# Two-layer hybrid transformer step with PEER experts: one lookup per pick for both expert tables, and gelu, gates and diagonal sums on TensorE in groups of four

## What is computed

```python
def one_chunk(xc):                       # 128 tokens, 1024 wide
    q = (xc @ wq).reshape(P_CHUNK, P_HEADS, 2, P_HALF)
    sc = jnp.einsum('thcd,hcnd->thcn', q, sub_keys)
    s1, i1 = lax.top_k(sc[:, :, 0], P_TOPK)
    s2, i2 = lax.top_k(sc[:, :, 1], P_TOPK)
    ...
    top_s, pos = lax.top_k(cand, P_TOPK)         # 8 heads x 16 picks of 16384 experts
    eidx = jnp.take_along_axis(cand_idx, pos, axis=-1)
    gate = jax.nn.softmax(top_s, axis=-1).astype(xc.dtype)
    u = jnp.take(u_tab, eidx, axis=0)
    act = jax.nn.gelu(jnp.einsum('thkd,td->thk', u, xc))
    vv = jnp.take(v_tab, eidx, axis=0)
    return jnp.einsum('thk,thkd->td', gate * act, vv)
```

## Time and profile before

| | |
|---|---|
| median of 3 runs | 2635.54 us |
| the profiled execution's own span | 2775.9 us |
| PE busy | 1502.5 us (54%) |
| DVE busy | 1580.1 us (57%) |
| ACT busy | 284.8 us (10%) |
| POOL busy | 1580.2 us (57%) |
| DMA moved | 963.23 MB, mean 347 GB/s |
| mean granted TensorE clock | 0.719 of full |

### The profile page before, as it was taken

The page is one execution under the profiler, slowest core; times in us unless marked ns, Lnnn a source line. Parts: engine busy times, 40 slices in busy tenths (PEclk is TensorE's granted clock), DMA queues, the critical chain, the costliest instruction groups (busy, mean ns, idle before and its releaser), DMA issues.

```text
span 2775.9 us, 21719 instructions
## 1 busy us (share of the span) xinstructions
PE 1502.5 (54%) x6476; PEld 657.2 (24%) x6476; DVE 1580.1 (57%) x3734; ACT 284.8 (10%) x736; POOL 1580.2 (57%) x1601
## 2 busy tenths in 40 slices
PE   6776766867626443445456776686642332232345
PEld 2254323424402111112222234333420000000011
DVE  1348958633767656647446578652668656547410
ACT  1211012211001001000000102211000000000000
POOL 0016526665555566664566785665556666666664
PEclk9888866788857765567777895788865656565567
DMA  9959987899899999998999997999979999999998
GB/s 362 387 204 392 370 310 270 306 371 364 309 381 353 395 357 359 357 353 320 349 369 404 338 391 275 327 333 354 363 292 376 363 359 348 356 364 358 362 372 305
DMA packets 299013, 963.23 MB, mean 347 GB/s; under 512 B 28280, under 2 KB 30712, under 8 KB 298128
## 3 DMA queue, kind: packets, MB, share of 16 engines
q0 software_dynamic: 221184, 805.40, 77.0%
q1 hardware_dynamic: 77712, 156.44, 15.5%
HBM read 959.12 MB, written 2.62 MB: 346 GB/s over the span
## 4 chain that ended last, share of the span: by engine, by line
PE 26%; DMA 19%; DVE 16%; issue 16%; POOL 11%; another core or an unknown queue 10%; ACT 1%; SPq 0%; POOLq 0%; DVEq 0%; ACTq 0%
POOL ring L815 11%; DMA ring<-peer_v,v_rows 9%; PE ps_acc L1095 8%; DVE ring L1663 8%; PE ps_mm L899 5%; DMA ring<-peer_u,u_rows 4%; PE ps_mm L1050 3%; DMA ring<-ada_w 2%; DMA weights<-w_in 2%; PE ps_mm L1020 2%; PE ps_mm L954 2%; DMA weights<-ada_w 1%; PE ps_mb L982 1%; PE ps_acc L858 1%
## 5 line engine op out<-in xcount | busy, mean ns | idle before, releaser
L815 POOL DMA_INDIRECT ring<-peer_v,v_rows x768 | 751.5, 978 | 588.2 <-issue 215.8
L815 POOL DMA_INDIRECT ring<-peer_u,u_rows x768 | 806.1, 1050 | 383.2 <-issue 207.3
L1095 PE MATMUL ps_acc<-ring,coef_cols 128*32 128x512 f32 x3072 | 589.0, 907 | 800.5 <-DMA ring<-peer_v,v_rows 785.8
L1663 DVE CUSTOM_DVE_ANT_0 ring<-ring,ps_tr 128x1024 f32<-128x1024 f32 x512 | 616.6, 1220 | 419.3 <-DMA ring<-peer_u,u_rows 347.8
L1095 PEld LDWEIGHTS ps_acc<-ring,coef_cols 128*32 128x32 f32 x3072 | 117.3, 143 | 1181.4 <-issue 1178.6
L1663 DVE CUSTOM_DVE_ANT_0 ring<-ring,h 128x1024 f32<-128x1024 f32 x256 | 304.9, 1221 | 24.0 <-DMA ring<-peer_u,u_rows 14.7
L1050 PE MATMUL ps_mm<-hT,weights 128*128 128x128 f32 (+1 forms) x1024 | 202.0, 353 | 23.9 <-issue 23.2
L899 PE MATMUL ps_mm<-weights,hT 128*128 128x512 f32 x432 | 199.0, 622 | 17.8 <-DMA weights<-w_in 13.4
L1050 PEld LDWEIGHTS ps_mm<-hT,weights 128*128 128x128 f32 x1024 | 170.8, 211 | 74.6 <-issue 61.4
L776 POOL TENSOR_SCALAR u_rows<-picks 128x16 uint32<-128x16 f32 x48 | 15.9, 330 | 204.2 <-DVE picks L1636 203.2
L899 PEld LDWEIGHTS ps_mm<-weights,hT 128*128 128x128 f32 x432 | 85.5, 200 | 130.8 <-issue 108.9
(11 more groups left out here) (218 smaller groups left out, 1525.9 us busy)
## 6 DMA issues: line engine op xcount, KB each, us to landing
weights<-w_in SPq DMA_DIRECT2D x17, 2048.0 KB
weights<-peer_wq SPq DMA_DIRECT2D x16, 2048.0 KB
weights<-ada_w SPq DMA_DIRECT2D x14, 2048.0 KB
ring<-ada_w SPq DMA_DIRECT2D x10, 2048.0 KB, 18.0
ring<-peer_u,u_rows POOLq DMA_INDIRECT x768
weights<-w_out SPq DMA_DIRECT2D x6, 2048.0 KB
ring<-peer_v,v_rows POOLq DMA_INDIRECT x768
ring<-w_in SPq DMA_DIRECT2D x3, 2048.0 KB, 20.7
```

What stands on the lines that cost most here:

```text
L815: pool.indirect_dma_start(ring[:, place % RING, :], None, src, bass.IndirectOffsetOnAxis(ap=rows, axis=0)).then_inc(row_full[place % RING] ...
L1095: last = pe.matmul(ps_acc[QROWS * k:QROWS * (k + 1), b * NB:(b + 1) * NB], coef_cols[:, i // PART % 2, at:at + QROWS], ring[:, slot("v", n ...
L1663: dve.tensor_tensor_reduce(row, row, h, 1.0, 0.0, ALU.mult, ALU.add, dots[:, n // UNIT % 2, n % UNIT:n % UNIT + 1]).then_inc(u_used, 1)
```

## The change

The tables u and v of a layer are put side by side in one array, 8 KB a row (`peer_uv0`, `peer_uv1`), outside the kernel. One indirect DMA a pick brings both rows, 768 in all, into a ring of 9 slots of 8 KB; the base, the turned picks and everything that made them go. Row numbers come from `route` as integers. Each v row now belongs to the same token as its partition. So for each pick ACT makes a diagonal of 128 x 128 from the identity, scaled by the coefficients, and PE adds the pick's rows with two matmuls of 128 columns against 512 (`add_rows`), without column tiles. A group of four picks goes through polynomial, tanh, coefficients, diagonals and adds in the step in which its dots are made. The dense work is dealt out by `sides()`, by ranges of picks: the rest of P0 and S0 up to the fifth query step in picks 0 to 103, S0's rest in 128 to 167, P1 in 168 to 351, S1 in 388 to 487, its rest in 512 to 551. Gates are exponentiated head by head and their sum's reciprocal goes into the coefficient; a tile is summed in one go. Seven late modulation chunks get their sums in another PSUM bank. The descriptor scratch shrinks from its default to 4096 bytes a partition.

The core of the diff, with what each engine does now in its own part:

```diff
+SLOTS = 9
...
+LATE_GROUPS = 0
+FEED_AT = 2
+DIAGS = 6
 AHEAD = 2
...
+def sides():
+
+    return ((0, 104, (Piece(P0, split_at(P_TILES), None, 2.5), Piece(S0, 0, split_at(S_TILES)))),
+            (TILE, TILE + 40, (Piece(S0, split_at(S_TILES)),)),
+            (TILE + 40, 3 * TILE - 32, (Piece(P1),)),
+            (3 * TILE + 4, 3 * TILE + 104, (Piece(S1, 0, split_at(S_TILES)),)),
+            (4 * TILE, 4 * TILE + 40, (Piece(S1, split_at(S_TILES)),)))
...
-        ring = sb("ring", [P, RING, DM])
-        coef_cols = sb("coef_cols", [P, 2, SPREAD])
+        ring = sb("ring", [P, SLOTS, 2 * DM])
+        diags = sb("diags", [P, DIAGS, P])
...
+            for n in range(PICKS):
+                if n % TOPK == 0:
+                    pool.wait_ge(picks_ready, n // TOPK + 1)
...
-                pool.indirect_dma_start(ring[:, place % RING, :], None, src,
-                                        bass.IndirectOffsetOnAxis(ap=rows, axis=0)).then_inc(row_full[place % RING], 16)
+                if n < RING_HOMES * HOME_SLOTS and n % HOME_SLOTS == 0:
+                    pool.wait_ge(*used(LATEST[WRING + n // HOME_SLOTS]))
+                    pool.sem_inc(gather_may, 1)
+                if n >= SLOTS:
+                    pool.wait_ge(v_used, n - SLOTS + 1)
+                    pool.sem_inc(gather_may, 1)
+                picks = rows[:, n // TOPK % HEADS_KEPT, n % TOPK:n % TOPK + 1]
+                pool.indirect_dma_start(ring[:, n % SLOTS, :], None, peer_uv1 if n >= PICKS // 2 else peer_uv0,
+                                        bass.IndirectOffsetOnAxis(ap=picks, axis=0)).then_inc(row_full[n % SLOTS], 16)
...
+            def add_rows(n):
+
+                tau, i = n // TILE, n % TILE
...
-                if i % PART == 0:
-                    pe.wait_ge(cols_ready, unit * PARTS + i // PART + 1)
-                n = unit * UNIT + i
-                for k in range(QUADS):
-                    pe.wait_ge(row_full[slot("v", n + k)], landed("v", n + k))
-                r = i // QUADS
+                    pe.wait_ge(mod_added, START_ADA)
+                    if tau:
+                        pe.wait_ge(acc_read, tau)
+                pe.wait_ge(diag_ready, n + 1)
                 for b in range(2):
-                    for k in range(QUADS):
-                        at = (k * PART // QUADS + r % (PART // QUADS) + 1) * QROWS - PER - PER * r
-                        last = pe.matmul(ps_acc[QROWS * k:QROWS * (k + 1), b * NB:(b + 1) * NB],
-                                         coef_cols[:, i // PART % 2, at:at + QROWS], ring[:, slot("v", n + k), b * NB:(b + 1) * NB],
-                                         start=(r == 0), stop=(r == UNIT // QUADS - 1), tile_position=(0, QROWS * k))
-                last.then_inc(v_used, QUADS)
+                    last = pe.matmul(ps_acc[:, b * NB:(b + 1) * NB], diags[:, n % DIAGS, :],
+                                     ring[:, n % SLOTS, DM + b * NB:DM + (b + 1) * NB], start=(i == 0), stop=(i == TILE - 1))
+                last.then_inc(v_used, 1)
...
-                pe.wait_ge(acc_added, tau + 1)
+                pe.wait_ge(acc_copied, tau + 1)
                 broadcast(ps_acc[:], tau // T, tau % T, GATE2).then_inc(gate2_bc, 1)
+
+            def add_group(g):
+                for k in range(GROUP):
+                    add_rows(g * GROUP + k)
...
+            start(programs)
+            side = Beside(programs)
+            for i in range(PICKS):
+                side.item(i)
+                if i % GROUP == GROUP - 1 and i // GROUP >= LATE_GROUPS:
+                    add_group(i // GROUP - LATE_GROUPS)
+                if i >= TILE and i % TILE == FEED_AT - 1:
+                    gate_sum_rows(i // TILE - 1)
+            for g in range(PICKS // GROUP - LATE_GROUPS, PICKS // GROUP):
+                add_group(g)
+            gate_sum_rows(DEPTH * T - 1)
...
+            def gate_exps(n):
+                act.wait_ge(gate_max, n + 1)
+                act.activation(gates_of(n), gates_of(n), ACT.Exp, bias=top_neg[:, n % 2:n % 2 + 1],
+                               accum_out=gate_sum[:, n % 2:n % 2 + 1]).then_inc(gate_exp, 1)
+
+            def gelu_tanh(g):
+                act.wait_ge(poly_ready, g + 1)
+                some = of_head(poly, g * GROUP, GROUP)
+                act.activation(some, some, ACT.Tanh, scale=GELU_B).then_inc(tanh_ready, 1)
+
+            def diagonals(g):
+                act.wait_ge(coef_ready, g + 1)
+                for n in range(g * GROUP, (g + 1) * GROUP):
+                    if n >= DIAGS:
+                        act.wait_ge(v_used, n - DIAGS + 1)
+                    act.activation(diags[:, n % DIAGS, :], ident, ACT.Copy, scale=of_head(coef, n)).then_inc(diag_ready, 1)
...
+            start(programs)
+            side = Beside(programs)
+            gate_exps(0)
+            for i in range(PICKS):
+                tau, j = i // TILE, i % TILE
+                if j == 0 and tau in SAMPLES and tau - 1 in SAMPLES:
+                    hold_rows(tau)
+                if i % GROUP == GROUP - 1:
+                    gelu_tanh(i // GROUP)
+                side.item(i)
+                if i % TOPK == 4 and i // TOPK + 1 < ALL_HEADS:
+                    gate_exps(i // TOPK + 1)
+                if i % GROUP == GROUP - 1:
+                    diagonals(i // GROUP)
...
+                dve.scalar_tensor_tensor(out=rows[:, n % HEADS_KEPT, :], in0=pair_key[:, 0], scalar=float(N_KEYS), in1=pair_key[:, 1],
                                          op0=ALU.mult, op1=ALU.add).then_inc(picks_ready, 1)
...
+            def polynomial(g):
+
+                n = g * GROUP
+                a, some = of_head(dots, n, GROUP), of_head(poly, n, GROUP)
+                dve.wait_ge(u_used, n + GROUP)
+                step.after(dve.scalar_tensor_tensor(out=some, in0=a, scalar=GELU_A, in1=a, op0=ALU.mult, op1=ALU.mult))
+                dve.scalar_tensor_tensor(out=some, in0=some, scalar=1.0, in1=a, op0=ALU.add, op1=ALU.mult).then_inc(poly_ready, 1)
+                if n % TOPK == 0:
+                    gate_scale(n // TOPK)
+                head, k = n // TOPK, n % TOPK
+                step.after(dve.scalar_tensor_tensor(out=of_head(gated, n, GROUP), in0=a, scalar=gate_inv[:, head % 2:head % 2 + 1],
+                                                    in1=gates_of(head)[:, k:k + GROUP], op0=ALU.mult, op1=ALU.mult))
+
+            def coefficients(g):
+
+                n = g * GROUP
+                dve.wait_ge(tanh_ready, g + 1)
+                dve.scalar_tensor_tensor(out=of_head(coef, n, GROUP), in0=of_head(poly, n, GROUP), scalar=1.0,
+                                         in1=of_head(gated, n, GROUP), op0=ALU.add, op1=ALU.mult).then_inc(coef_ready, 1)
...
+                if k == TOPK // 2:
+                    for _ in routing:
+                        pass
+                    routing = route(head + AHEAD) if head + AHEAD < ALL_HEADS else iter(())
+                next(routing, None)
+                if k == 2 and head + 1 < ALL_HEADS:
+                    gate_top(head + 1)
+                dot(i)
+                if i % GROUP == GROUP - 1:
+                    polynomial(i // GROUP)
+                side.item(i)
+                if i % GROUP == GROUP - 1:
+                    coefficients(i // GROUP)
+                if i >= TILE and i % TILE == FEED_AT:
+                    feed(i // TILE - 1)
+            feed(DEPTH * T - 1)
...
+    for l in range(DEPTH):
+        arrays[f"peer_uv{l}"] = np.concatenate([a["peer_u"][l], a["peer_v"][l]], axis=1)
...
+    nc = bacc.Bacc("TRN2", target_bir_lowering=False, num_devices=1, dynamic_dma_scratch_size=4096)
```

More of the change, by code:

```diff
@@ L95, in split_at @@
     return len(steps(tiles)) - 16 + FIRST_PQ
-def after_out(tiles):
-    return steps(tiles).index("out") + OUT_CHUNKS * len(tiles)
-SPARSE = 2 * QUADS
-EARLY, LATE = (0, UNIT // 2), (UNIT // 2, UNIT)
 GELU_A = 0.044715
@@ L160, in __init__ @@
         self.weights = [weight or weights[kind] for kind in kinds[first:last]]
-class Beside:
-    def __init__(self, pieces, programs, items):
-        self.steps = [(programs[piece.stage], weight) for piece in pieces for weight in piece.weights]
-        self.share = sum(weight for _, weight in self.steps) / items
-        self.due, self.done, self.at = 0.0, 0, 0
-    def step(self):
-        program, weight = self.steps[self.at]
-        next(program)
-        self.done += weight
-        self.at += 1
-    def item(self):
-        self.due += self.share
-        while self.at < len(self.steps) and self.done < self.due - 1e-6:
-            self.step()
-    def end(self):
-        while self.at < len(self.steps):
-            self.step()
@@ new lines, with __init__, item @@
+class Beside:
+    def __init__(self, programs):
+        self.programs, self.at = programs, [0] * len(sides())
+        self.done = [0.0] * len(sides())
+    def item(self, i):
+        for s, (first, end, pieces) in enumerate(sides()):
+            if not first <= i < end:
```

(18 more changed lines are left out.)

449 lines of the change are left out of this document (67 added, 382 removed).

## The result

The changed kernel takes 3029.23 us (3024.06 to 3030.38, 4 runs) beside 2634.32 us before: 1.150 times as long, 95% interval 1.147 to 1.152. The forecast was 2950 us, slower, within 2640 to 3240. Its profiled execution took 3028.4 us with a span of 3026.6, so here profile and median agree; the kernel before had a profile 140 us above its median, and the last experiment comes back to that.

The account below looks back on a forecast made before the run. The DMA was taken to bound the kernel before, TensorE the dense sample stages after. 205 + 572 + 308 + 608 + 519 + 855 + 25 = 3092 us profiled, less 140, say 2950 us; range 2640 to 3240.

Parts of the forecast that it names:

- Price of a group: Full-width adds of four picks on TensorE: 8.1 us a group, between 7.06 and 14.1 by clock level.
- The coupling: TensorE's wait in every group for diagonals from its own dots: 2.5 us with sample tiles, 2 with P1's.
- (1): Picks 0 to 103 beside the rest of P0 and S0: 572 us, bound by TensorE; DMA alone 399.
- (3): Picks 168 to 351 beside P1: 608 us, two equal bounds colliding, TensorE's 588 and DMA's 587.
- (4): Picks 388 to 487 beside S1: 519 us, DMA 341.
- Steps of queries: Twice 40 picks beside eleven query steps: 154 us each, 308 together.
- Bare picks: 300 picks without dense work beside them: 2.85 us each, 855 us, with 2.3% gained by long rows.
- The sum: Whole kernel: 3092 us in profiled time, less the 140 by which before's profile exceeded its median, say 2950.
- POOL, slots: Lookup queue: halving 1536 lookups frees POOL, counted as nothing more; nine slots keep four lookups, 4.2 MB, under way: enough.
- (a): Whole kernel: DMA keeps its lead, exposed waits vanish, TensorE gets the upper clock; about 2560 us, chance 0.17.
- (b): TensorE's clock stays low, mean 0.64, a group of adds costs 11 us; 3300 us, chance 0.11.
- (c): Bare picks: long rows bring nothing or cost, 2.91 us each, +18 us; inside the range, no separate chance given.

Follow-up runs that it names:

- e4: Changed kernel with each group's four dots and coefficients made ahead of its dense steps, adds still at the fourth step; 2778.3 us.
- e9: Changed kernel with groups of two picks for four and the adds one pair late; 2686.5 us.
- e2: Kernel before with each packed add of four v rows issued four times, sums wrong by that; 3131.5 us.
- e3: Changed kernel with the tables apart, two lookups of 4 KB rows a pick into the halves of the same slot; 3055.3 us.
- e10: e9's kernel run again for an interval; 2690.0 us, ratio 0.968 to the kernel before beside it.
- e12: Kernel before, unchanged, profiled again; 2780.2 us.
- e6: e4 with seven slots of 8 KB for nine; 3186.9 us.
- e1: Changed kernel with one matmul a pick for two, leaving out the second half of every expert sum; 2776.2 us.
- e11: e9 with each pair's two v rows folded into one ahead of TensorE, beside P0/S0 and beside S1 only; 2732.0 us.

## Why the prediction was right, and where not

Direction and mechanism held: the stretches in which adds and dense work share TensorE's order turned from DMA-bound to bound by TensorE and its waits. Point by point, in profiled time:

- **Price of a group.** 8.1 us forecast; 1550.5 / 192 = 8.08 on the mean of all groups. In the three dense stages it was 8.4, 8.1 and 8.5, somewhat more than forecast. With more clock the mean was 7.69 in e4 and 7.56 in e9, still above the bound of 7.06. The factor of four over column tiles that the earlier trace rows gave held (e2's four packed adds a group, 1504 us in all, against 1550). The Trainium skill ("TensorE: Matmul & The Clock Gate", Part 3) states its packing gain of 3.07 for four row tiles, and the tiles here are column tiles; the estimate from it, 5.6 us a group at the upper level, was too cheap: at a granted clock of 0.99 a group took 7.3 us (72.8 us for ten, picks 128 to 167).
- **The coupling.** 2.5 and 2 us a group forecast; 77.6 / 26 = 3.0, 68.5 / 25 = 2.7 and 122.1 / 42 = 2.9. The place was right and the size somewhat small. The forecast took dots, polynomial and tanh to be done before TensorE gets there; in the group shown above two dots were still to come. What the forecast didn't see is what hangs on the wait: e4 and e9 took off 251 and 343 us, not the 220 that 26 x 2.5 + 46 x 2 + 25 x 2.5 gives. The gaps also go with a lower clock, and they keep slots. A diagonal took 1.27 / 4 = 0.32 us, as put down.
- **Stages.** 572 us forecast against 600 for (1), 608 against 630 for (3), 519 against 526 for (4): 57 us low together. These near hits owe something to luck, since larger errors cancel. In (1) and (4) the dense matmuls took 247 and 209 us, not 286 and 243; the forecast had carried over the times of before, at a clock of 0.77 and 0.81, where 0.83 and 0.87 were granted now. Against that, adds and waits for diagonals came to 21 and 15 us more than put down; and the rest of TensorE's idle time, mostly waits for weights, for VectorE and for ScalarE inside the dense program, took 56 and 35 us where 10 stood. Of the terms of the stages that one was the furthest off. TensorE was busy 78% of (1), short of the "over 80%" that was to show it, and 80.3% of (4), at DMA shares under 0.75 as said.
- **Steps of queries.** Twice 133 against 154. I took 8.1 us a group there too, but the stretch was granted 0.99: ten groups took 73 us and not 81, the query steps 46 and not 53. Of the 20 us of waits 15 came.
- **Bare picks.** 2.85 us forecast, 2.56 measured over the last 215, and 775 us for all 300 against 855. The long rows are worth 2.2% (e3), as good as the 2.3% that I took. The other tenth is between a profile of the kernel before at its upper level and one of the new kernel; how much of it the one queue and its order of release bring, and how much belongs to the level, was not separated.
- **The sum.** 3092 us forecast for the profiled execution, 3028 measured, 2% high. The 57 us too little in the stages stood against 42 too much in the query steps and 80 in the bare picks, so the closeness of the sum is luck in part. The step that failed is the last one, the 140 us taken off because before's profile lay that far above its median. I carried an offset of one execution over to another kernel; the new kernel's profile is at its median. Without it the forecast would have been 3092 us, 63 too high, instead of 79 too low. That the offset belongs to the kernel before and to the occasion is what e10 and e12 show.
- **POOL, slots.** Half as many lookups, waiting on TensorE: as said. "Enough" for nine slots is shown in the bare stretch only (share 0.99); with two fewer it is no longer so (e6, 0.87).
- **Rivals.** (a), the DMA keeping its lead: 0.67 and 0.62 in the dense stages rule it out, and 0.82 and 0.77 are the most that the scheme reached there, with the wait gone (e9). (b), a low clock: 0.83 to 0.99 granted. (c) is out by e3.

From the 3 cycles a packet that the Trainium skill states ("DMA: Bandwidth & Descriptors", Why small descriptors are slow) the forecast estimated a gain of 1.1% for rows of 8 KB; e3 against the kernel after shows 2.2%, for row length and number of lookups together.

## What to carry to other kernels

An operand made from the same step's data puts the producer's whole chain into the consumer's order: let the consumer use the one made a step earlier, and shrink the group so that the delay needs no more buffers. Here that was two constants, and 343 of the 395 us by which the change was behind at the lower level. Price an add both ways, what it takes of its engine and how long it holds the slot that feeds the next transfer. And don't carry the difference between a profiled run and a median over to another kernel.

## What the runs showed of the hardware

- Work taken from TensorE went with a lower clock: half the adds (e1), mean clock 0.886 to 0.807, 664 to 823 ns a record; 14% fewer records in a stage (e11), 0.92 to 0.83. Waits taken away went with a higher one: 0.886 to 0.944 (e9).
- Lookups of 8 KB rows reach 404 to 413 GB/s at a share of 0.99 to 1.00, of 4 KB rows 396 at 1.00 (e3), and 358 and 360 at 0.96 in the kernel before.
- In this ring two slots of nine were worth 409 us (e6 against e4), 15% of the run, and the bare stretch fell from a share of 1.00 to 0.87.
- Four column tiles of 32 side by side took about a quarter of the time of four full-width adds: 1504 us for four times the packed adds (e2, mean clock 0.87), 1550 us for the unpacked ones once (0.89).
- The same program, unchanged, took 2630 us at one time (one run) and 2766 to 2799 us at another (23 runs) on one chip. Another kernel with the same data, e9's, took 2687 us beside the one level and 2690 us beside the other.
